# One mixer and expert layer in float32: the expert stage's weight ring re-mapped at its start, the down matrix fetched by output columns, the gate begun on quarters, the last norm taken per column block

## The chip, the cores and the metric

The kernel runs on one core of a Trainium2 chip, in one launch. The metric is the device time of that core in microseconds (us). All numbers are float32. TensorE (PE in the tables) multiplies, VectorE (DVE) and ScalarE (ACT) do the elementwise work, SyncE (SP) issues nearly all transfers.

## What is computed

One layer on 256 tokens of width 2048: a token mixer (a state-space branch and a gated delta-rule branch), a layer norm, then 32 experts of hidden width 512, of which each token takes 4, and a second layer norm.

```python
h = layer_norm(DEEPNORM_ALPHA * h + mix, ln1_g, ln1_b)
logits = h @ w_router + b_router
top_val, top_idx = lax.top_k(logits, 4); top_w = softmax(top_val)
...
gate = jnp.minimum(xb @ w_gate[e] + b_gate[e], 7.0)
up = jnp.clip(xb @ w_up[e] + b_up[e], -7.0, 7.0)
y = (gate * sigmoid(1.702 * gate) * (up + 1.0)) @ w_down[e] + b_down[e]
...
h = layer_norm(DEEPNORM_ALPHA * h + ffn, ln2_g, ln2_b)
```

The expert weights are w_gate and w_up (32 x 2048 x 512) and w_down (32 x 512 x 2048), some 403 MB, each used once.

## The kernel before

The program is written engine by engine, with semaphores between them. The mixer fills the first two thirds of the time. The change touches only the stage after it.

**The expert stage** takes the experts in 16 pairs (`PAIRS`). If no expert has more than 64 tokens (`CAP`; the flag read on every engine, `over < 1`, which holds for these inputs), each pair is done on 64 + 64 token slots, one expert in columns 0 to 63 of the array and the other in columns 64 to 127. A float32 matmul of the code is two MATMUL instructions in the trace; the counts here are of instructions. PE's order for pair i is in `sparse(i)`:

- `sgate`: two small matmuls (four instructions) lay the biases into banks 0 and 1, then `expand(0, 0, i)` multiplies by w_gate in four steps of 16 instructions (L1108);
- `sup`: `expand(1, 4, i)`, the same with w_up;
- `gather(i + 1)`: the tokens of the next pair are picked by 64 instructions (L1086) into banks 4 to 7, which ACT copies to `xg` in four quarters (`sgather`, L1454);
- `scatter(i - 1, 0, 6)`: six of the eight matmuls (two instructions each, L1165) that spread the last pair's outputs to the tokens, added to `acc` by DVE (L2050);
- `turn_hidden` (L1128), the last two scatters, `turn_weights` (L1133): transposes that ACT copies to `shT` and `pwT` (`sturn`);
- `sdown`: four steps of 16 instructions (L1142). Step k multiplies a quarter of the hidden width and adds to all four output banks, so that all banks finish in step 3; ACT then copies them to `ysb` (L1474).

In pair 0 the scatter carries b_down too (`bias_part`, L1035), and it runs in pair 1.

**The weights** come in units of 2 MB: twelve a pair (`PER_PAIR`), j = 0 to 3 of w_gate, 4 to 7 of w_up, 8 to 11 of w_down. A unit holds both experts: two rows of 2048 numbers in each of 128 partitions. Six places (`unit[0..5]`, `UNITS`) form a ring. For pair 0 there are three more, `extra`, which take j = 6, 7 and 8, so that nine units are loaded before the stage begins. From then on SP reloads in the order in which PE reads: j = 9, 10, 11 of pair 0, then all of pair 1, and so on. Unit j goes to place j % 6, and `reload_unit` waits until that place's last user was read:

```python
sp.wait_ge(unit_read[j % UNITS], 2 * i + j // UNITS - (1 if j % UNITS < 3 else 0))
```

Since SP works in order, a unit whose place isn't free holds back all later ones. PE releases a place behind the last matmul that reads it (`last.then_inc(read, 1)`).

**The end.** After the last pair's `sdown` come its eight scatters, four column blocks of token tile 0 and then four of tile 1. DVE adds each block (L2069) and takes its statistics (L2071); behind each tile `spread` makes mean, variance and reciprocal (L1866 to L1871), ACT the square root (L1402). Then DVE normalises each tile with a pass over 2048 columns (L2090) and two over 1024 (L2095), and SP stores each half (L503).

Of the kernel before, what the change touches and what calls it, by code (L numbers as in the profile page):

```python
# [12 lines left out]
ALU = mybir.AluOpType  # L13
ACT = mybir.ActivationFunctionType
# [55 lines left out]
def build(nc, x, w_in, conv_w, a_log, dt_bias, norm_w, w_dn, lam_re, lam_im, log_dt, b_re, b_im, c_re, c_im,  # L70
# [3 lines left out]
    with ExitStack() as ctx:  # L74
# [139 lines left out]
        def lnv(m, i):  # L214
            return small[:, 64 + 8 * m + i:65 + 8 * m + i]

        def top8(m, i):
            return small[:, 80 + 16 * m + 8 * i:88 + 16 * m + 8 * i]

# [55 lines left out]
        p_built, xg_done, xg_taken, y_copied, sc_done, sc_taken, sdn_done = (  # L275
            sem("p_built"), sem("xg_done"), sem("xg_taken"), sem("y_copied"), sem("sc_done"), sem("sc_taken"),
            sem("sdn_done"))
# [27 lines left out]

        def tile_rows(w):
            return w.rearrange("(k p) n -> p k n", p=P)

        block = ctx.enter_context(nc.Block())

# [2 lines left out]
        def _(sp):  # L313
# [117 lines left out]
            def load_extra(j):  # L431
                sp.dma_start(extra[j - UNITS], unit_source(j, 0)).then_inc(extra_loaded[j - UNITS], 16)
# [171 lines left out]
        def _(pe):  # L604
# [485 lines left out]
            def await_unit(j, i):  # L1090
                if isinstance(i, int) and i == 0 and UNITS <= j < UNITS + 3:
                    pe.wait_ge(extra_loaded[j - UNITS], 16)
                    return extra[j - UNITS], extra_read
                b = j % UNITS
                if isinstance(i, int) and i == 0:
                    pe.wait_ge(unit_loaded[b], 16 * (j // UNITS) + 16)
                else:
                    pe.wait_ge(unit_loaded[b], 32 * i + 16 * (j // UNITS) + (0 if b < 3 else 16))
# [26 lines left out]
            def turn_hidden(i):  # L1125
                pe.wait_ge(hb_ready, i + 1)
                for k in range(KF):
                    last = tr(ps[4][:, k * P:k * P + P], shb[:, k::KF], ident[:, :])  # L1128
                last.then_inc(htr_ready, 1)

            def turn_weights(i):
                for m in range(MT):
                    last = tr(ps[5][:, m * P:m * P + P], Pw[:, m].rearrange("p o c -> p (o c)"), ident[:, :])  # L1133
                last.then_inc(htr_ready, 1)

            def sdown(i):
                pe.wait_ge(htr_taken, 2 * i + 2)
                for k in range(KF):
                    buf, read = await_unit(8 + k, i)
                    for n in range(4):  # L1140
                        for o in range(2):
                            last = mm(ps[4 + n][CAP * o:CAP * o + CAP, :], shT[:, k, CAP * o:CAP * o + CAP],  # L1142
                                      buf[:, o, n * 512:n * 512 + 512], start=k == 0, stop=k == KF - 1)
                        if k == KF - 1 and n < 3:
                            last.then_inc(sdn_done, 1)
                    last.then_inc(read, 1)

            def scatter(i, lo, hi, more=True):
                if lo == 0:
                    pe.wait_ge(y_copied, 4 * i + 4)  # L1150
                    if more:
                        pe.wait_ge(up_taken, i + 2)
                    else:
                        pe.wait_ge(sc_taken, 8 * i)
# [15 lines left out]
            def sparse(i, first=False, more=True):  # L1170

                sgate(i)
                sup(i)
                if first:
                    turn_wt()
                if more:
                    gather(i + 1)
                if not first:
                    scatter(i - 1, 0, 6)
                pe.wait_ge(xg_taken, 4 * i + (8 if more else 4))  # L1180
                turn_hidden(i)
# [9 lines left out]
            with pe.If(over < 1):  # L1191
# [5 lines left out]
                scatter(PAIRS - 1, 0, 8, more=False)  # L1197
            with pe.If(over > 0):
                turn_tokens()
                turn_wt()  # L1200
# [11 lines left out]
        def _(act):  # L1212
# [254 lines left out]

            def sdown(i):
                for n in range(4):
                    if n < 3:  # L1470
                        act.wait_ge(sdn_done, 3 * i + n + 1)
                    else:
                        act.wait_ge(unit_read[5], 2 * i + 2)
# [20 lines left out]
            with act.If(over > 0):  # L1494
# [4 lines left out]
                    hidden(e)  # L1499
                    turn(e - 1)  # L1500
                turn(N_E - 1)
            for m in range(MT):
                root(m, MT + m)


        @block.vector
        def _(dve):
# [511 lines left out]
                    V.tensor_tensor(av, av, ps[6 + n % 2][:, :], ALU.add).then_inc(dn_taken[n % 2], 1)  # L2019

            def stake_gate(i):
                dve.wait_ge(unit_read[3], 2 * i + 1)
# [4 lines left out]
            def stake_up(i):  # L2027
                if isinstance(i, int) and i == 0:
                    dve.wait_ge(extra_read, 2)
                else:  # L2030
                    dve.wait_ge(unit_read[1], 2 * i + 1)
# [21 lines left out]
            with dve.If(over < 1):  # L2053
# [11 lines left out]
                for m in range(MT):  # L2065
                    for n in range(4):
                        av = acc[:, m, 512 * n:512 * n + 512]
                        dve.wait_ge(sc_done, 8 * (PAIRS - 1) + 4 * m + n + 1)
                        V.tensor_tensor(av, av, ps[(2, 3, 0, 1)[n]][:, :], ALU.add).then_inc(sc_taken, 1)  # L2069
                        dve.drain()  # L2070
                        V.bn_stats(stats[:, 24 * m + 6 * n:24 * m + 6 * n + 6], av)  # L2071
                    spread(m, 24 * m, 24 * m + 24)
            with dve.If(over > 0):
                add_down(-1)
                take_gate(0)
# [7 lines left out]
                for m in range(MT):  # L2083
                    for n in range(4):
                        V.bn_stats(stats[:, 24 * m + 6 * n:24 * m + 6 * n + 6], acc[:, m, 512 * n:512 * n + 512])
                    spread(m, 24 * m, 24 * m + 24)
            dve.wait_ge(ln2_loaded, 32)
            for m in range(MT):
                dve.wait_ge(root_ready, MT + m + 1)
                V.scalar_tensor_tensor(out=acc[:, m], in0=acc[:, m], scalar=lnv(m, MU), in1=ln2row[:, 0],  # L2090
                                       op0=ALU.subtract, op1=ALU.mult)
                dve.drain()
                for h in range(2):
                    half = slice(D // 2 * h, D // 2 * h + D // 2)
                    V.scalar_tensor_tensor(out=acc[:, m, half], in0=acc[:, m, half], scalar=lnv(m, RSTD),  # L2095
# [26 lines left out]
```

## Time and profile before

| | us |
|---|---|
| median of three runs | 2986.1 (2983.25 to 2987.63) |
| the profiled execution's own time | 2986.08 |
| its span in the profile | 2984.3 |
| PE busy, share of the span | 97% |
| DVE, ACT busy | 31%, 17% |
| data moved by transfers | 654.05 MB |
| expert stage, from the first expert gather to the end of the span | 1993.5 to 2984.3 |

The profile gives times from the start of the span. Busy shares are averages over stages with different limits, and matmul ends are modelled. "Idle before, releaser" names what ended an engine's idle time. The chain of waits is followed back from the last instruction to what released each step. The share of DMA is the time that packets took on the 16 transfer engines, which can come out a little over 1.

### The profile page before, as it was taken

To read this page: it belongs to the slowest core of one execution; us is meant where nothing else is said; L and a number is where in the kernel's file an instruction comes from. 1 tells how busy PE (TensorE), PEld (TensorE's weight loads), DVE (VectorE), ACT (ScalarE), POOL (GpSimd) and SP (SyncE) were. 2 spreads that over 40 slices of the span, in tenths; PEclk is the share of its full clock that TensorE was granted. 3 is DMA by queue.
4 is the path that set the end of the run, shared out by engine and by line. 5 is a ranking of instruction groups with operands and counts; after the bars stand their busy time and mean duration, and the time that the engine had idled before them with its cause. 6 is when DMAs were issued, how large, how long until landed. Compare 5 with 4: busy or idle time off the path is not lost.

```text
span 2984.3 us, 47457 instructions
## 1 busy us (share of the span) xinstructions
PE 2900.1 (97%) x19639; PEld 2086.5 (70%) x19639; DVE 912.0 (31%) x2066; ACT 517.6 (17%) x809; POOL 100.5 (3%) x179
## 2 busy tenths in 40 slices
PE   8999999999999999999999999999999999999996
PEld 7888788888888888888888888873444444444442
DVE  1433424424334307777730000130121112111214
ACT  2221222222212132111010000121111111112110
POOL 2010011000100000000000000000000000000000
PEclk9999999999999999999999999999999999999998
DMA  6243342332434524244347665258899999999996
GB/s 195 81 131 99 98 125 91 101 123 80 138 94 113 154 95 136 92 127 128 122 145 218 197 194 171 112 204 361 362 422 422 422 422 422 422 422 422 422 422 261
DMA packets 325775, 654.05 MB, mean 219 GB/s; under 512 B 45232, under 2 KB 274736, under 8 KB 275440
## 3 DMA queue, kind: packets, MB, share of 16 engines
q1 hardware_dynamic: 325616, 651.61, 59.4%
q8 instruction: 139, 2.28, 0.3%
q14 instruction: 20, 0.16, 0.0%
HBM read 649.49 MB, written 2.10 MB: 218 GB/s over the span
## 4 chain that ended last, share of the span: by engine, by line
PE 58%; issue 16%; DVE 12%; DMA 6%; DVEq 2%; ACT 1%; POOLq 1%; POOL 1%; SPq 1%; ACTq 0%
PE bank L938 11%; PE bank L632 10%; PE bank L1108 9%; PE bank L1142 7%; DMA arena<-in_w_up_dram 6%; DVE arena L1759 4%; PE bank L1086 4%; PE bank L972 4%; PE bank L1165 4%; DVE arena L1761 3%; DVE arena L1763 3%; PE bank L706 1%; PE bank L724 1%; PE bank L717 1%; PE bank L1119 1%
## 5 line engine op out<-in xcount | busy, mean ns | idle before, releaser
L632 PE MATMUL bank<-arena 128*128 128x256 f32 x4096 | 934.0, 383 | 0.0
L632 PEld LDWEIGHTS bank<-arena 128*128 128x128 f32 x4096 | 765.3, 190 | 112.6 <-issue 8.0
L1108 PE MATMUL bank<-arena 128*64 128x512 f32 x2048 | 447.0, 595 | 6.2 <-DMA arena<-in_w_up_dram 6.2
L1108 PEld LDWEIGHTS bank<-arena 128*64 128x64 f32 x2048 | 145.1, 137 | 306.1 <-issue 290.1
L938 PE MATMUL bank<-arena 128*128 128x256 f32 x1536 | 331.8, 379 | 0.0
L938 PEld LDWEIGHTS bank<-arena 128*128 128x128 f32 x1536 | 291.8, 190 | 39.9 <-issue 0.3
L1142 PE MATMUL bank<-arena 128*64 128x512 f32 x1024 | 223.3, 594 | 7.7 <-ACT masks L1466 7.7
L877 PE MATMUL bank<-arena 128*128 128x256 f32 x1024 | 223.5, 380 | 0.0
L877 PEld LDWEIGHTS bank<-arena 128*128 128x128 f32 x1024 | 194.0, 190 | 27.3 <-issue 1.0
L1142 PEld LDWEIGHTS bank<-arena 128*64 128x64 f32 x1024 | 72.1, 137 | 148.5 <-issue 137.0
L2023 DVE TENSOR_SCALAR arena<-bank 128x512 f32<-128x512 f32 x16 | 11.1, 692 | 473.7 <-PE bank L1108 473.7
L1454 ACT ACTIVATE arena<-bank,small 128x128 f32<-128x128 f32 x256 | 96.2, 456 | 224.5 <-PE bank L1086 224.5
L1759 DVE TENSOR_TENSOR arena<-arena 128x256 f32<-128x256 f32 x256 | 124.2, 485 | 32.5 <-issue 15.5
L1086 PEld LDWEIGHTS bank<-arena 128*128 128x128 f32 x1024 | 116.9, 194 | 12.1 <-issue 11.4
L1086 PE MATMUL bank<-arena 128*128 128x128 f32 x1024 | 119.8, 278 | 0.7 <-ACTq L1410 0.7
L1165 PE MATMUL bank<-arena,masks 128*128 128x512 f32 x256 | 117.0, 596 | 2.5 <-DVEq L2037 1.8
L2050 DVE TENSOR_TENSOR arena<-arena,bank 128x512 f32<-128x512 f32 x120 | 82.4, 688 | 105.2 <-PE bank L1165 105.0
L972 PE MATMUL bank<-arena 128*128 128x256 f32 x512 | 114.0, 381 | 0.0
L1551 DVE TENSOR_SCALAR arena<-bank,cw 128x256 f32<-128x256 f32 x64 | 28.0, 480 | 256.5 <-PE bank L632 255.8
L972 PEld LDWEIGHTS bank<-arena 128*128 128x128 f32 x512 | 96.2, 190 | 12.5
L1761 DVE TENSOR_TENSOR arena<-arena 128x128 f32 x256 | 82.8, 323 | 43.5 <-issue 43.5
L1557 DVE SCALAR_TENSOR_TENSOR arena<-bank,cw,arena 128x255 f32<-128x255 f32 (+2 forms) x192 | 83.7, 477 | 16.5 <-issue 16.4
(307 smaller groups left out, 2001.4 us busy)
## 6 DMA issues: line engine op xcount, KB each, us to landing
arena<-in_w_in_dram SPq DMA_DIRECT2D x72, 2048.0 KB, 8.7
arena<-in_w_up_dram SPq DMA_DIRECT2D x64, 2048.0 KB, 15.9
arena<-in_w_gate_dram SPq DMA_DIRECT2D x64, 2048.0 KB, 13.4
arena<-in_w_down_dram SPq DMA_DIRECT2D x64, 2048.0 KB, 20.6
arena<-in_w_dn_out_dram SPq DMA_DIRECT2D x16, 2048.0 KB, 8.5
arena<-in_w_glu_b_dram SPq DMA_DIRECT2D x8, 2048.0 KB, 8.2
arena<-in_w_glu_a_dram SPq DMA_DIRECT2D x8, 2048.0 KB, 8.3
arena<-in_w_mix_out_dram SPq DMA_DIRECT2D x8, 2048.0 KB, 13.7
```

The lines of the kernel that those rows point to most:

```text
L632: last = mm(ps[bank][:, ct * T:ct * T + T], ring[:, buf, k, ct * P:ct * P + P], rhs[:, k, :], start=k == 0, stop=k == KD - 1)
L877: last = mm(ps[bank][:, ct * T:ct * T + T], ring[:, n % 2, k, ct * P:ct * P + P], oT[:, half * KD + k, :], start=half == 0 and ct == 0 and ...
L938: last = mm(ps[3 - 3 * odd + b][:, ct * T:ct * T + T], ring[:, buf, k, ct * P:ct * P + P], rhs[:, k, :], start=k == 0, stop=k == KD - 1)
L972: last = mm(ps[bank][:, 0:SC], mg[:, k, m * P:m * P + P], mixw[r][:, k, :], start=k == 0, stop=k == KD - 1)
L1086: last = mm(ps[4 + b][:, k * P:k * P + P], h1[:, m, 4 * b + k], Psel[:, m].rearrange("p o c -> p (o c)"), start=m == 0, stop=m == MT - 1)
L1108: last = mm(ps[bank][CAP * o:CAP * o + CAP, :], xg[:, 4 * q + k, CAP * o:CAP * o + CAP], w[:, o, k], start=False, stop=q == 3 and k == 3, ...
L1142: last = mm(ps[4 + n][CAP * o:CAP * o + CAP, :], shT[:, k, CAP * o:CAP * o + CAP], buf[:, o, n * 512:n * 512 + 512], start=k == 0, stop=k ...
L1165: last = mm(ps[bank][:, :], pwT[:, (n // 4) * P:(n // 4) * P + P], ysb[:, (n % 4) * 512:(n % 4) * 512 + 512], start=not biased, stop=True, ...
L1454: last = A(xg[:, k, :], ps[4 + b][:, P * j:P * j + P], ACT.Identity, scale=gqk[:, k:k + 1], bias=bqk[:, k:k + 1])
L1759: V.tensor_tensor(prod, prev.unsqueeze(2).to_broadcast([P, 2, 2, NJ]), rot, ALU.mult)
L1761: V.tensor_tensor(cur, cur, prod[:, 0], ALU.add)
L1763: V.tensor_tensor(cur, cur, prod[:, 1], ALU.add)
```

## The change

Four edits, all in the expert stage and its end.

1. **Places.** `place_of(j, i)` and `earlier_uses(j, i)` take the place of `j % UNITS` and of the two counts, on SP, PE, DVE and ACT. Units 9, 10, 11 of pair 0 go to places 0, 1, 2 (before 3, 4, 5), and unit j of every later pair to (j + 3) % 6.
2. **The down matrix.** Unit 8 + n of w_down holds 512 output columns, n * 512 and on, of all 512 hidden rows, where it held a quarter of the hidden rows with all 2048 columns. `sdown` is `down_columns(i, n)` for n = 0 to 3: 16 instructions into bank 4 + n alone. ACT's copy of a bank waits for that unit's release (`sdn_done` is gone). The first step waits for `shT` alone, the others for `pwT` too. The hidden transposes read contiguous columns (`shb[:, k * P:...]`).
3. **The gate** waits for the quarters of `xg` one by one, and the bias matmuls before it for none.
4. **The end.** In the last pair `scatter_columns(i, n)` stands behind `down_columns(i, n + 1)`: the two token tiles of one column block. DVE takes the blocks in that order, then makes the statistics of both tiles in one go (`ln_pair`), and the first normalising pass starts before the square root is there.

```diff
+        def place_of(j, i):
+            if isinstance(i, int) and i == 0:
+                return j if j < UNITS else j - UNITS - 3
+            return (j + 3) % UNITS
+
+        def earlier_uses(j, i):
+            if isinstance(i, int) and i == 0:
+                return 0 if j < UNITS else 1
+            return 2 * i + j // UNITS - (0 if place_of(j, i) < 3 else 1)
...
                 if kind == 2:
-                    return w_down[ds(2 * i, 2)].rearrange("o (p k) n -> p o k n", k=KF)[:, :, quarter, :]
+                    return (w_down[ds(2 * i, 2)].rearrange("o (k p) n -> p (o k) n", p=P)
+                            [:, :, F_E * quarter:F_E * quarter + F_E])
...
             def load_unit(j, i):
-                sp.dma_start(unit[j % UNITS], unit_source(j, i)).then_inc(unit_loaded[j % UNITS], 16)
+                b = place_of(j, i)
+                to = unit[b] if j < 8 else unit[b].rearrange("p o (k n) -> p (o k) n", k=KF)
+                sp.dma_start(to, unit_source(j, i)).then_inc(unit_loaded[b], 16)
...
-                sp.wait_ge(unit_read[j % UNITS], 2 * i + j // UNITS - (1 if j % UNITS < 3 else 0))
+                sp.wait_ge(unit_read[place_of(j, i)], earlier_uses(j, i))
...
             def expand(bank, first, i):
                 for q in range(4):
                     j = first + q
+                    if bank == 0:
+                        pe.wait_ge(xg_taken, 4 * i + q + 1)
...
             def sgate(i):
-                pe.wait_ge(xg_taken, 4 * i + 4)
...
-                    last = tr(ps[4][:, k * P:k * P + P], shb[:, k::KF], ident[:, :])
+                    last = tr(ps[4][:, k * P:k * P + P], shb[:, k * P:k * P + P], ident[:, :])
...
+            def down_columns(i, n):
+                pe.wait_ge(htr_taken, 2 * i + 1 + (n > 0))
+                buf, read = await_unit(8 + n, i)
+                w = buf.rearrange("p o (k n) -> p o k n", k=KF)
+                for k in range(KF):
+                    for o in range(2):
+                        last = mm(ps[4 + n][CAP * o:CAP * o + CAP, :], shT[:, k, CAP * o:CAP * o + CAP], w[:, o, k],
+                                  start=k == 0, stop=k == KF - 1)
+                last.then_inc(read, 1)
+
             def sdown(i):
-                pe.wait_ge(htr_taken, 2 * i + 2)
...
+            def scatter_columns(i, n):
+
+                pe.wait_ge(y_copied, 4 * i + n + 1)
+                for m in range(MT):
+                    j = 2 * n + m
+                    pe.wait_ge(sc_taken, 8 * i + max(j - 3, 0))
+                    mm(ps[(2, 3, 0, 1)[j % 4]][:, :], pwT[:, m * P:m * P + P], ysb[:, n * 512:n * 512 + 512],
+                       start=True, stop=True).then_inc(sc_done, 1)
...
                 turn_weights(i)
-                sdown(i)
+                if more:
+                    sdown(i)
+                else:
+                    down_columns(i, 0)
+                    for n in range(1, 4):
+                        down_columns(i, n)
+                        scatter_columns(i, n - 1)
+                    scatter_columns(i, 3)
...
+            dve.drain()
+            for m in range(MT):
+                V.bn_aggr(small[:, 64 + 8 * m + MU:64 + 8 * m + MU + 2], stats[:, 24 * m:24 * m + 24])
+            dve.drain()
+            V.tensor_scalar(ln_pair(RINV), ln_pair(VAR), LN_EPS, None, ALU.add)
+            dve.drain()
+            V.reciprocal(ln_pair(RINV), ln_pair(RINV))
```

On SP the first reloads of the stage stood like this before (L432 is unit 8 of pair 0, L429 the reloads of units 9, 10, 11 of pair 0; `unit3_free` and its like are the counts of reads of a place; the last figures are partitions x pieces x numbers in a piece):

```order
L432 DMA arena<-in_w_down_dram 128x2x2048 [waits resid_done]
L469 TENSOR_LOAD flag [waits flag_ready]
L469 ISA x2
L470 COMPARE_AND_BRANCH
L429 DMA arena<-in_w_down_dram 128x2x2048 [waits unit3_free]
L429 DMA arena<-in_w_down_dram 128x2x2048 [waits unit4_free]
L429 DMA arena<-in_w_down_dram 128x2x2048 [waits unit5_free]
```

and now:

```order
L448 DMA arena<-in_w_down_dram 128x8x512 [waits resid_done]
L485 TENSOR_LOAD flag [waits flag_ready]
L485 ISA x2
L486 COMPARE_AND_BRANCH
L444 DMA arena<-in_w_down_dram 128x8x512 [waits unit0_free]
L444 DMA arena<-in_w_down_dram 128x8x512 [waits unit1_free]
L444 DMA arena<-in_w_down_dram 128x8x512 [waits unit2_free]
```

The three reloads wait for places that are read three units sooner, and each piece in memory is 512 numbers (2 KB) instead of 2048 (8 KB), eight in a partition instead of two.

On PE the last pair ended like this before (L1133 is `turn_weights`, L1142 `sdown`, L1165 the scatter):

```order
L1133 MATMUL bank<-ident,arena 128x128 x2
L1142 MATMUL bank<-arena 64x512 [waits unit2_loaded,htr_taken]
L1142 MATMUL bank<-arena 64x512 x7
L1142 MATMUL bank<-arena 64x512 [waits unit3_loaded]
L1142 MATMUL bank<-arena 64x512 x7
L1142 MATMUL bank<-arena 64x512 [waits unit4_loaded]
L1142 MATMUL bank<-arena 64x512 x7
L1142 MATMUL bank<-arena 64x512 [waits unit5_loaded]
L1142 MATMUL bank<-arena 64x512 x7
L1165 MATMUL bank<-arena,masks 128x512 [waits sc_taken,y_copied]
L1165 MATMUL bank<-arena,masks 128x512 x3
L1165 MATMUL bank<-arena,masks 128x512 [waits sc_taken] x4
```

and now, from its second column block on (L1156 is `down_columns`, L1170 `scatter_columns`):

```order
L1156 MATMUL bank<-arena 64x512 [waits unit0_loaded,htr_taken]
L1156 MATMUL bank<-arena 64x512 x7
L1170 MATMUL bank<-arena,masks 128x512 [waits sc_taken,y_copied]
L1170 MATMUL bank<-arena,masks 128x512 [waits sc_taken]
L1156 MATMUL bank<-arena 64x512 [waits unit1_loaded,htr_taken]
L1156 MATMUL bank<-arena 64x512 x7
L1170 MATMUL bank<-arena,masks 128x512 [waits sc_taken,y_copied]
L1170 MATMUL bank<-arena,masks 128x512 [waits sc_taken]
```

Six of the eight scatters have moved ahead of the end: two stand behind the second, the third and the last down step each, and two more at the very end.

## Rows read from the trace of the kernel before

**Rows 1.** The page, part 2: the span in 40 slices of 74.6 us.

```profile
PE   8999999999999999999999999999999999999996
PEclk9999999999999999999999999999999999999998
DMA  6243342332434524244347665258899999999996
GB/s 195 81 131 99 98 125 91 101 123 80 138 94 113 154 95 136 92 127 128 122 145 218 197 194 171 112 204 361 362 422 422 422 422 422 422 422 422 422 422 261
```

**Rows 2.** The chain of waits, 2360 to 2460: start us, us, what.

```profile
2366.13 7.04 PE bank L1108 x32
...
2373.31 17.56 DMA arena<-in_w_up_dram
...
2390.92 3.65 PE bank L1108 x16
...
2432.98 17.59 DMA arena<-in_w_up_dram
```

**Rows 3.** Stretches: from:to, length, busy times, granted clock, DMA share, GB/s.

```profile
1622.00:1630.00 8.00, 8.00 (x39) 7.04 (x38) 0.00 (x0) 0.00 (x0) 0.00 (x0) 1.00 1.09 351
...
2056.00:2108.00 52.00, 52.00 (x238) 21.29 (x234) 7.89 (x18) 8.98 (x21) 0.00 (x0) 1.00 1.01 422
2108.00:2118.00 10.00, 9.54 (x33) 3.58 (x34) 2.13 (x4) 0.96 (x2) 0.00 (x0) 1.00 0.18 75
2120.00:2900.00 780.00, 768.70 (x3704) 328.49 (x3702) 130.31 (x273) 130.39 (x301) 0.00 (x0) 1.00 1.01 422
```

**Rows 4.** SP's instructions in order of time: start us, us, line, what.

```profile
2021.89 6.89 SPq L429 DMA_DIRECT2D arena<-in_w_down_dram  x3
2029.21 24.48 SPq L429 DMA_DIRECT2D arena<-in_w_gate_dram  x4
```

**Rows 5.** PE in order of time, pairs 0 to 3.

```profile
1993.54 8.75 PE L1086 MATMUL bank<-arena 128*128 128x128 f32 x64 [0.67 <-ACTq L1410]
2003.88 1.98 PE L1119 MATMUL bank<-arena,masks 32*128 32x512 f32 x4 [1.59 <-ACT arena L1454]
...
2045.99 13.96 PE L1142 MATMUL bank<-arena 128*64 128x512 f32 x64 [0.73 <-ACT masks L1466]
...
2114.82 13.95 PE L1142 MATMUL bank<-arena 128*64 128x512 f32 x64 [0.46 <-ACT masks L1466]
...
2187.54 1.98 PE L1119 MATMUL bank<-arena,masks 32*128 32x512 f32 x4
...
2246.39 1.98 PE L1119 MATMUL bank<-arena,masks 32*128 32x512 f32 x4
```

**Rows 6.** Issue to landing, least/median/most: L432 at 2001.7 (8 KB pieces).

```profile
DMA to landing us min/median/max: 7.5/7.5/7.5
```

**Rows 7.** The same for L366, 1087 to 1500 (24 transfers, 1 KB pieces).

```profile
DMA to landing us min/median/max: 8.1/8.6/9.7
```

**Rows 8.** PE in order of time, the end.

```profile
2928.06 3.65 PE L1108 MATMUL bank<-arena 128*64 128x512 f32 x16 [0.87 <-DMA arena<-in_w_up_dram]
...
2941.78 13.95 PE L1142 MATMUL bank<-arena 128*64 128x512 f32 x64 [0.46 <-ACT masks L1466]
2956.42 7.16 PE L1165 MATMUL bank<-arena,masks 128*128 128x512 f32 x16 [0.69 <-ACT arena L1474]
```

**Rows 9.** DVE in order of time, the end.

```profile
2957.58 0.69 DVE L2069 TENSOR_TENSOR arena<-arena,bank 128x512 f32<-128x512 f32 x1 [15.76 <-PE bank L1165]
...
2958.97 0.67 DVE L2069 TENSOR_TENSOR arena<-arena,bank 128x512 f32<-128x512 f32 x1
...
2969.83 0.26 DVE L1866 BATCH_NORM_AGGREGATE small<-small 128x2 f32<-128x24 f32 x1
...
2971.40 2.35 DVE L2090 SCALAR_TENSOR_TENSOR arena<-arena,small 128x2048 f32<-128x2048 f32 x1 [0.78 <-ACTq L1402]
```

More of the change, by code:

```diff
@@ L215, in lnv, with ln_pair @@
             return small[:, 64 + 8 * m + i:65 + 8 * m + i]
+        def ln_pair(i):
+            return small[:, 64:80].rearrange("p (m i) -> p m i", i=8)[:, :, i]
         def top8(m, i):
@@ L274, in build @@
         sel_ready, pos_ready, flag_ready = sem("sel_ready"), sem("pos_ready"), sem("flag_ready")
-        p_built, xg_done, xg_taken, y_copied, sc_done, sc_taken, sdn_done = (
-            sem("p_built"), sem("xg_done"), sem("xg_taken"), sem("y_copied"), sem("sc_done"), sem("sc_taken"),
-            sem("sdn_done"))
+        p_built, xg_done, xg_taken, y_copied, sc_done, sc_taken = (
+            sem("p_built"), sem("xg_done"), sem("xg_taken"), sem("y_copied"), sem("sc_done"), sem("sc_taken"))
         x_loaded = [sem(f"x_tile{m}_loaded") for m in range(MT)]
@@ L428, in load_unit @@
             def load_unit(j, i):
-                sp.dma_start(unit[j % UNITS], unit_source(j, i)).then_inc(unit_loaded[j % UNITS], 16)
+                b = place_of(j, i)
+                to = unit[b] if j < 8 else unit[b].rearrange("p o (k n) -> p (o k) n", k=KF)
+                sp.dma_start(to, unit_source(j, i)).then_inc(unit_loaded[b], 16)
             def load_extra(j):
-                sp.dma_start(extra[j - UNITS], unit_source(j, 0)).then_inc(extra_loaded[j - UNITS], 16)
+                to = extra[j - UNITS] if j < 8 else extra[j - UNITS].rearrange("p o (k n) -> p (o k) n", k=KF)
+                sp.dma_start(to, unit_source(j, 0)).then_inc(extra_loaded[j - UNITS], 16)
             def reload_unit(j, i):
-                sp.wait_ge(unit_read[j % UNITS], 2 * i + j // UNITS - (1 if j % UNITS < 3 else 0))
+                sp.wait_ge(unit_read[place_of(j, i)], earlier_uses(j, i))
                 sp.sem_inc(load_free, 1)
@@ L1093, in await_unit @@
                     return extra[j - UNITS], extra_read
[L1094 to L1098, printed above, removed]
+                b = place_of(j, i)
+                pe.wait_ge(unit_loaded[b], 16 * earlier_uses(j, i) + 16)
                 return unit[b], unit_read[b]
@@ L1134, in turn_weights, with scatter @@
                 last.then_inc(htr_ready, 1)
-            def sdown(i):
-                pe.wait_ge(htr_taken, 2 * i + 2)
[L1138 to L1148, printed above, removed]
+            def down_columns(i, n):
[7 more added lines that the diff above has]
+                last.then_inc(read, 1)
+            def sdown(i):
+                for n in range(4):
+                    down_columns(i, n)
[6 more added lines that the diff above has]
+                       start=True, stop=True).then_inc(sc_done, 1)
+            def scatter(i, lo, hi):
                 if lo == 0:
                     pe.wait_ge(y_copied, 4 * i + 4)
[L1151 to L1154, printed above, removed]
+                    pe.wait_ge(up_taken, i + 2)
                 biased = isinstance(i, int) and i == 0
@@ L1184, in sparse @@
                 turn_weights(i)
-                sdown(i)
+                if more:
[3 more added lines that the diff above has]
+                    for n in range(1, 4):
+                        down_columns(i, n)
+                        scatter_columns(i, n - 1)
+                    scatter_columns(i, 3)
             pe.wait_ge(xhat_done, MT)
@@ L1196, in _ @@
                 sparse(PAIRS - 1, more=False)
-                scatter(PAIRS - 1, 0, 8, more=False)
             with pe.If(over > 0):
@@ L1469, in sdown @@
                 for n in range(4):
-                    if n < 3:
-                        act.wait_ge(sdn_done, 3 * i + n + 1)
+                    if isinstance(i, int) and i == 0 and n == 0:
+                        act.wait_ge(extra_read, 3)
                     else:
-                        act.wait_ge(unit_read[5], 2 * i + 2)
+                        act.wait_ge(unit_read[place_of(8 + n, i)], earlier_uses(8 + n, i) + 1)
                     nc.scalar.copy(ysb[:, n * 512:n * 512 + 512], ps[4 + n][:, :]).then_inc(y_copied, 1)
@@ L1501, in _ @@
                 turn(N_E - 1)
-            for m in range(MT):
-                root(m, MT + m)
+            act.wait_ge(rv_ready, MT + 1)
+            A(ln_pair(RSTD), ln_pair(RINV), ACT.Sqrt)
+            act.drain()
+            act.sem_inc(root_ready, 1)
         @block.vector
@@ L2021, in stake_gate @@
             def stake_gate(i):
-                dve.wait_ge(unit_read[3], 2 * i + 1)
+                dve.wait_ge(unit_read[place_of(3, i)], earlier_uses(3, i) + 1)
                 V.tensor_scalar(sgb, ps[0][:, :], LIMIT, None, ALU.min)
@@ L2030, in stake_up @@
                 else:
-                    dve.wait_ge(unit_read[1], 2 * i + 1)
+                    dve.wait_ge(unit_read[place_of(7, i)], earlier_uses(7, i) + 1)
                 V.tensor_scalar(shb, ps[1][:, :], LIMIT, -LIMIT, ALU.min, ALU.max)
@@ L2064, in _ @@
                 add_scatter(PAIRS - 2)
-                for m in range(MT):
-                    for n in range(4):
+                for n in range(4):
+                    for m in range(MT):
+                        j = 2 * n + m
                         av = acc[:, m, 512 * n:512 * n + 512]
-                        dve.wait_ge(sc_done, 8 * (PAIRS - 1) + 4 * m + n + 1)
-                        V.tensor_tensor(av, av, ps[(2, 3, 0, 1)[n]][:, :], ALU.add).then_inc(sc_taken, 1)
+                        dve.wait_ge(sc_done, 8 * (PAIRS - 1) + j + 1)
+                        V.tensor_tensor(av, av, ps[(2, 3, 0, 1)[j % 4]][:, :], ALU.add).then_inc(sc_taken, 1)
                         dve.drain()
                         V.bn_stats(stats[:, 24 * m + 6 * n:24 * m + 6 * n + 6], av)
-                    spread(m, 24 * m, 24 * m + 24)
             with dve.If(over > 0):
@@ L2085, in _ @@
                         V.bn_stats(stats[:, 24 * m + 6 * n:24 * m + 6 * n + 6], acc[:, m, 512 * n:512 * n + 512])
-                    spread(m, 24 * m, 24 * m + 24)
+            dve.drain()
+            for m in range(MT):
+                V.bn_aggr(small[:, 64 + 8 * m + MU:64 + 8 * m + MU + 2], stats[:, 24 * m:24 * m + 24])
[3 more added lines that the diff above has]
+            V.reciprocal(ln_pair(RINV), ln_pair(RINV))
+            dve.drain()
+            dve.sem_inc(rv_ready, 1)
             dve.wait_ge(ln2_loaded, 32)
             for m in range(MT):
-                dve.wait_ge(root_ready, MT + m + 1)
                 V.scalar_tensor_tensor(out=acc[:, m], in0=acc[:, m], scalar=lnv(m, MU), in1=ln2row[:, 0],
@@ L2092, in _ @@
                 dve.drain()
+                if m == 0:
+                    dve.wait_ge(root_ready, MT + 1)
                 for h in range(2):
```

## The prediction

> **What bounds the kernel now.** I read the page's slices first. In the last third, from the 29th slice on, the transfers run at 422 GB/s in every full slice, while PE is also busy nine tenths [rows 1]: two resources are near their limit, and the page can't say which sets the pace. The chain of waits can. Once in each pair it leaves PE for some 17.6 us and goes over a transfer of w_up: 2373.31, then 2432.98, so once in 59.67 us [rows 2]. Twelve units at 422 GB/s are 12 x 2.097 MB / 422 = 59.63 us: the pair lasts as long as its weights take to arrive. PE alone needs less. In an early pair, in which it waits for no transfer, it goes from one bias step to the next in 2246.39 - 2187.54 = 58.85 us [rows 5]. So the stage is bound by the transfers, and PE has 0.8 us of slack in a pair. Whatever makes the stream of weights longer is paid in full; whatever makes PE shorter is lost, but at the two ends.
>
> Where does the stream begin to bind? The stretches show it full from 2056 to 2108, nearly idle from 2108 to 2118 (share 0.18), and then full at 422 GB/s to 2900 [rows 3]. The hole is there because PE is late: pair 1 has the scatter with b_down, its down step begins only at 2114.82 [rows 5], and unit 2 of pair 2 needs the place that the first down unit of pair 1 gives back some 3.5 us later. From this point 162 units (10 of pair 2, 12 in each of pairs 3 to 14, 8 of pair 15) flow without a hole to PE's last wait for a transfer, at 2928.06 [rows 8]. Behind it comes the tail, which is PE and DVE alone: last down step, scatters, statistics, norm.
>
> So the time is the restart of the stream, plus 162 units, plus the tail. Each edit is put to these three terms. The sum is made against the profiled execution, 2986.08 us (span 2984.3); the median of the runs is 2986.1, so the difference carries over unchanged.
>
> **Places: 0.** Units 9 to 11 of pair 0 were issued at 2021.89, when unit 3 had been read [rows 4]. They now wait for unit 0, three steps earlier: the 16 instructions of a step take 3.5 us (13.96 / 4) [rows 5], so 10.5 us sooner. But units 0, 1, 2 of pair 1 come next [rows 4], and behind them unit 3, which needs unit 9's place, before and after alike, and that is read only in pair 0's down step. The stream, sooner or later, stands at this point. Nothing in pair 0 or 1 waited for a transfer (the idle before its steps is for ACT [rows 5]), so the earlier arrival has no taker. What covers it is the hole of 2108 to 2118, about 8 us of idle transfers; were it gone, up to 10.5 us would count, a rival below.
>
> **Gate on quarters, first down step without pwT: -2.4 us on the restart.** PE stood 1.59 us before the first bias matmul at 2003.88, for ACT's last quarter [rows 5]; the bias no longer waits and takes 1.9 us, in which that quarter is copied: -1.6. The down step waited 0.73 us in pair 0 and 0.46 in pair 1 for the copy to `pwT` [rows 5]. In pair 0 the copy to `shT` stands just ahead of it and still has to be awaited, so I take -0.3; in pair 1 -0.5. PE reaches pair 1's down step 2.4 us sooner and the stream restarts 2.4 us sooner. In pairs 2 to 14 the same 0.5 us is hidden by the transfers, as is a gate wait that had long been met.
>
> **Down units of 2 KB pieces: +22.4 us on the stream.** A unit was 256 pieces of 8 KB, 16 for each of 16 engines; now it is 1024 pieces of 2 KB, 64 for each. No large transfer in this trace has 2 KB pieces, so I bound it from both sides of the size. With 8 KB the stream holds 422 GB/s: a piece costs 16 x 8192 / 422 = 310.6 ns. With 1 KB (w_glu and w_mix, queued behind each other) it holds 351 GB/s [rows 3]: 16 x 1024 / 351 = 46.7 ns. The line through both is 9.0 ns a piece plus 0.0368 ns a byte; 2 KB then cost 84.4 ns, a unit 64 x 84.4 = 5.40 us against 16 x 310.6 = 4.97, so +0.43 us. Transfers that run alone are the further bound: 7.5 us with 8 KB [rows 6], 8.1 to 9.7 (most often 8.6) with 1 KB [rows 7], for 112 pieces more per engine. The 48 more of a 2 KB unit would be 48/112 of 0.6 to 2.2 us, 0.26 to 0.94 us. A gain is not excluded by a row, but both sizes put the larger piece ahead; the bound below is 0. I take 0.43, from full-rate rows like those of this stage. Of the 162 units 4 in each of pairs 2 to 14 are down units: 52 x 0.43 = +22.4. Those of pairs 0 and 1 (8 x 0.43 = 3.4 us) fall into the hole, those of pair 15 lie behind the last wait, where PE reaches each some 4 us after it has landed. The Trainium skill says otherwise: DMA: Bandwidth & Descriptors, Specifications, puts full rate at transfers of 512 B and more, by which 2 KB pieces would be free.
>
> SP's issues stay as many, and the 16 instructions of a step keep their shape: 0. With 61.4 us a pair PE's slack grows to some 3 us, so ACT's copies, now spread over the down steps, wait for nobody.
>
> **The tail: -4.9 us.** Before, from the down step at 2941.78 [rows 8] to the first normalising pass at 2971.40 [rows 9]. Now: down starts 0.5 us sooner, 2941.3. Four steps are 13.9 us; two pairs of scatters stand among them, and the eight scatters took 7.16 us, 0.86 each without the last one's drain [rows 8], so 4 x 0.86 = 3.4; the last step ends at 2958.6. The scatters of block 2 follow at once, while ACT copies block 3. DVE took its first block 1.16 us behind the first scatter (2957.58 against 2956.42), and a block, add and statistics, takes 1.39 us (2958.97 - 2957.58), longer than a scatter [rows 8, 9]. DVE has four blocks left where it had eight: 2958.6 + 1.2 + 5.6 = 2965.4. From aggregation to reciprocal it is for one tile 2971.40 - 2969.83 less 0.78 for the root, 0.8 [rows 9], plus 0.3 for the second tile: the first pass starts at 2966.5. The root is made under that pass of 2.35 us [rows 9]. 2966.5 - 2971.4 = -4.9; the passes and stores behind it are the same.
>
> **Sum.** -2.4 + 22.4 - 4.9 = +15.1 us: 2986.1 + 15.1 = **3001.2 us**.
>
> **The rivals.**
> - *Pieces of 2 KB are free.* Each engine would have enough in its queue to hide what a piece costs beyond its bytes. Then -2.4 - 4.9 = -7.3: 2978.8 us, faster. It decides below 7.3 / 52 = 0.14 us a unit, 79.9 ns a piece. This is what the page's 512 B would give. Against it: full queues of 1 KB pieces, half that size, hold 351 GB/s and not 422 [rows 3]. For it: none of the rows is of 2 KB. Chance 0.17.
> - *Most of it hidden, not all*: 0.14 to 0.26 us a unit, between that point and the lower bound of the lone transfers, +0 to +6.2: 2986 to 2992. Chance 0.08.
> - *The early reloads carry through*: the hole closes, since the stream has more of a lead than I read from the ring, and the 10.5 us of the first reloads count at the end. +15.1 - 10.5 = +4.6: 2990.7. Against it is the wait for unit 9's place, in both orders. Chance 0.06.
> - *Rows 8 KB apart cost memory time too.* A piece is now one quarter of a matrix row, and a unit touches 1024 rows. With the most that lone 1 KB transfers took, 0.94 us, 52 x 0.94 - 7.3 = +41.6: 3027.7 us. Beyond 0.65 us (3012.6) I call it this case. Against it: the 351 GB/s are of matrices whose rows are 8 KB apart as well. Chance 0.10. The Trainium skill, DMA: Bandwidth & Descriptors, Latency and other measured facts, reports such losses for row pitches from 2 MiB up; no row here shows one.
> - *The edit is not what it says*: the order of SP shows 128x8x512, so the transfers are cut as the diff has it; only a joining of pieces in hardware could undo this, which is the first rival.
>
> **How the numbers follow.** The forecast, 0.26 to 0.65 us a unit (+6.2 to +26.5, 2992 to 3013), has 0.59. The range reaches down into the free case and a little into the dear one, and leaves out some 0.1 of the former and 0.07 of the latter: 2979 to 3015. A measurement of this kernel can tell about 0.2%, 6 us. Faster by more than that needs less than 0.03 us a unit: 0.13 of the first rival's 0.17. Within it: the rest, 0.04, the half-hidden case 0.08 and the early reloads 0.06, together 0.18. Slower: 0.59 + 0.10 = 0.69.
>
> **What would show it.** Right: full stretches of the stage near 410 GB/s (12 units in 61.35 us), a period of some 61.4 us between the w_up waits in the chain, PE's wait per pair grown from under 1 to some 3 us; the hole before pair 1's down step still there; PE's last wait at about 2928 + 20 = 2948; the first normalising pass 4.4 us nearer to the last down step. Wrong: 422 GB/s and 59.7 us a pair (pieces are free), no hole near 2110 (the early reloads count), or under 400 GB/s (rows cost).

## The result and the profile after

Five runs of the changed kernel have a median of 3000.87 us (2999.21 to 3001.55); the kernel before, five runs, 2983.25 us (2981.47 to 2987.63). The ratio is 1.0056, 95% interval 1.0041 to 1.0071: slower, by 17.6 us of the medians. The forecast was 3001.2 us and slower, +15.1.

The page of the kernel after, its first line and its slices of 75 us, answers to [rows 1]:

```profile
span 2999.1 us, 47575 instructions
...
PE   8999999999999999999999999999999999999997
...
DMA  7233242242334534334347665268999999999997
GB/s 206 85 114 113 86 141 85 86 141 85 113 113 100 154 100 129 111 113 141 113 141 225 199 209 178 101 245 346 365 411 412 408 405 412 412 411 405 408 412 285
```

Where 422 GB/s stood in every full slice there are now 405 to 412. The busy share of the transfer engines is as high as before: they work as much and bring less.

The chain of waits of the kernel after, 2360 to 2460 (start us, us, what), against [rows 2]:

```profile
2373.97 19.91 DMA arena<-in_w_up_dram
...
2393.93 3.65 PE bank L1123 x16
...
2435.42 19.89 DMA arena<-in_w_up_dram
...
2455.36 3.65 PE bank L1123 x16
```

The wait for w_up ends at 2393.93 and again at 2455.36: a pair is 61.43 us, where it was 59.67.

The stretches of the kernel after (columns as in [rows 3]):

```profile
2108.00:2118.00 10.00, 10.00 (x43) 3.38 (x44) 1.38 (x2) 1.19 (x3) 0.00 (x0) 1.00 0.26 83
2120.00:2900.00 780.00, 750.22 (x3611) 317.40 (x3608) 126.91 (x269) 127.11 (x295) 0.00 (x0) 1.00 1.03 409
```

The hole before pair 1's down step is still there, and behind it 409 GB/s take the place of 422. PE's busy time in the same 780 us fell from 768.70 to 750.22 us: it waits. In the kernel before, 5.3 us of PE's waits in this stretch ended with a transfer of w_up and 6.0 with ACT's copy to `pwT`; now it is 29.8 us, all for w_up.

PE in order of time, kernel after, first pairs, against [rows 5], and the end, against [rows 8]:

```profile
1990.99 9.86 PE L1102 MATMUL bank<-arena 128*128 128x128 f32 x64 [0.47 <-DVEq L1989]
2000.79 1.98 PE L1133 MATMUL bank<-arena,masks 32*128 32x512 f32 x4
...
2040.82 15.50 PE L1156 MATMUL bank<-arena 128*64 128x512 f32 x64 [0.46 <-ACT arena L1492]
...
2110.63 13.95 PE L1156 MATMUL bank<-arena 128*64 128x512 f32 x64
...
2942.30 3.65 PE L1123 MATMUL bank<-arena 128*64 128x512 f32 x16 [1.31 <-DMA arena<-in_w_up_dram]
2947.28 3.65 PE L1123 MATMUL bank<-arena 128*64 128x512 f32 x16 [1.32 <-DMA arena<-in_w_up_dram]
...
2960.43 7.09 PE L1156 MATMUL bank<-arena 128*64 128x512 f32 x32
...
2978.44 3.70 PE L1170 MATMUL bank<-arena,masks 128*128 128x512 f32 x8
```

Four of these starts cut the stage into the three terms of the forecast. *Start* is from the first gather to pair 1's down step, where the stream of weights restarts. *Stream* is from there to PE's last wait for a transfer. *Tail* is from there to the end of the span.

| us | before | after | difference | forecast |
|---|---|---|---|---|
| start | 2114.82 - 1993.54 = 121.28 | 2110.63 - 1990.99 = 119.64 | -1.6 | -2.4 |
| stream | 2928.06 - 2114.82 = 813.24 | 2947.28 - 2110.63 = 836.65 | +23.4 | +22.4 |
| tail | 2984.3 - 2928.06 = 56.24 | 2999.1 - 2947.28 = 51.82 | -4.4 | -4.9 |
| sum | 990.76 | 1008.11 | +17.35 | +15.1 |

What lies ahead of the first gather is the same code in both and differed by 2.6 us between these two executions; over all runs shown below the first gather began between 1987.8 and 1996.2. A difference of single executions carries that scatter, which is why the terms are read inside the stage.

DVE in order of time, kernel after, against [rows 9]:

```profile
2979.61 0.69 DVE L2100 TENSOR_TENSOR arena<-arena,bank 128x512 f32<-128x512 f32 x1 [2.65 <-PE bank L1170]
...
2985.27 0.39 DVE L2118 BATCH_NORM_AGGREGATE small<-small 128x2 f32<-128x24 f32 x2
...
2986.27 2.35 DVE L2127 SCALAR_TENSOR_TENSOR arena<-arena,small 128x2048 f32<-128x2048 f32 x1
```

Four blocks of 1.4 us are left when the last two scatter pairs arrive, and the first normalising pass follows the aggregation at once: no idle time for the root stands before it, as it did in [rows 9].

### The profile page after: what moved, and what is told of

It reads as the page before. It is cut to its first block, busy times and chain, and to the rows that moved or that the text cites. A ratio compares the mean times of both kernels' runs of the same rounds, so it can differ in the third digit from the quotient of the medians.

```text
span 2999.1 us, 47575 instructions
## 1 busy us (share of the span) xinstructions
PE 2902.9 (97%) x19639; PEld 2083.3 (69%) x19639; DVE 912.3 (30%) x2062; ACT 517.3 (17%) x808; POOL 100.5 (3%) x179
## 4 chain that ended last, share of the span: by engine, by line
PE 56%; issue 16%; DVE 12%; DMA 9%; DVEq 2%; POOLq 1%; POOL 1%; ACT 1%; SPq 1%; ACTq 0%
PE bank L954 11%; PE bank L648 10%; DMA arena<-in_w_up_dram 9%; PE bank L1156 7%; PE bank L1123 7%; DVE arena L1789 4%; PE bank L1102 4%; PE bank L988 4%; PE bank L1187 3%; DVE arena L1791 3%; DVE arena L1793 3%; PE bank L722 1%; PE bank L740 1%; PE bank L733 1%; PE bank L1133 1%
## 5 line engine op out<-in xcount | busy, mean ns | idle before, releaser
L1156 PE MATMUL bank<-arena 128*64 128x512 f32 x1024 | 225.2, 597 | 0.5 <-ACT arena L1492 0.5
L1156 PEld LDWEIGHTS bank<-arena 128*64 128x64 f32 x1024 | 72.1, 138 | 142.0 <-issue 141.3
L1102 PEld LDWEIGHTS bank<-arena 128*128 128x128 f32 x1024 | 118.0, 195 | 11.9 <-issue 11.4
L1187 PE MATMUL bank<-arena,masks 128*128 128x512 f32 x240 | 109.8, 596 | 1.8 <-DVEq L2067 1.8
```

The costliest lines, as they stand in the source:

```text
L1102: last = mm(ps[4 + b][:, k * P:k * P + P], h1[:, m, 4 * b + k], Psel[:, m].rearrange("p o c -> p (o c)"), start=m == 0, stop=m == MT - 1)
L1187: last = mm(ps[bank][:, :], pwT[:, (n // 4) * P:(n // 4) * P + P], ysb[:, (n % 4) * 512:(n % 4) * 512 + 512], start=not biased, stop=True, ...
```

## The experiments

The theory: the loss is a fixed time for each piece of a down unit, paid in 52 units; start and tail keep small gains. Its rivals: PE's new order or new waits; rows far apart; a threshold in the piece size; early reloads that hid part of the loss. Each run is told by its ratio to the kernel before on the same chip. The stream term of each is read from its own trace, as in the table above.

**e1: the change with whole rows.**

```diff
                 if kind == 2:
-                    return (w_down[ds(2 * i, 2)].rearrange("o (k p) n -> p (o k) n", p=P)
-                            [:, :, F_E * quarter:F_E * quarter + F_E])
+                    return w_down[ds(2 * i, 2)].rearrange("o (p k) n -> p o k n", k=KF)[:, :, quarter, :]
...
-                to = unit[b] if j < 8 else unit[b].rearrange("p o (k n) -> p (o k) n", k=KF)
+                to = unit[b]
...
```

> The changed kernel, but each down unit is fetched in whole rows of 8 KB again (the transfers of the kernel before), while PE, ACT and DVE do what the change has them do. The weights so multiplied are not the reference's. Theory (the piece size costs 0.43 us a down unit, 52 of them on the path): 22 us less than the changed kernel, ratio to before about 0.9976 (some 2976 to 2979 us where before is 2983), 422 GB/s and 59.7 us a pair. Rival (the time comes from PE's new order, its new waits or the new places): stays near 3001 us.

Measured: 2976.52 us, ratio 0.9969 (0.9957 to 0.9981). PE, stretch and end of this run:

```profile
2120.00:2900.00 780.00, 768.15 (x3705) 327.17 (x3702) 130.31 (x273) 130.78 (x302) 0.00 (x0) 1.00 1.01 422
```

```profile
2114.01 11.38 PE L1155 MATMUL bank<-arena 128*64 128x512 f32 x52
...
2927.36 3.65 PE L1122 MATMUL bank<-arena 128*64 128x512 f32 x16 [1.31 <-DMA arena<-in_w_up_dram]
```

The stream is 2927.36 - 2114.01 = 813.35 us, as before the change (813.24). Every instruction of PE, ACT and DVE is the change's; the source and destination patterns of the down units' transfers are not. So the whole loss is in how the down units are fetched, and the rest of the change is faster than the kernel before.

**e3: the columns alone, on the kernel before.** `unit_source`, the two destinations, the transposes, `sdown` and ACT's waits for it are as in the change; places, gate and end are the old ones, and the down step still waits for both copies.

```diff
             def sdown(i):
                 pe.wait_ge(htr_taken, 2 * i + 2)
-                for k in range(KF):
-                    buf, read = await_unit(8 + k, i)
...
+                for n in range(4):
+                    buf, read = await_unit(8 + n, i)
+                    w = buf.rearrange("p o (k n) -> p o k n", k=KF)
```

> The kernel before with the down matrix by output columns and nothing else of the change: old places, gate behind all four quarters, both copies awaited before the down step, old end. Theory: 52 x 0.43 = 22.4 us more than before, some 3005 to 3007 us, ratio 1.0075. The tail and the start give nothing. Rival (part of the loss comes from the other edits): less than 17 us more.

Measured: 3007.76 us, ratio 1.0075 (1.0061 to 1.0088), which is 22.6 us over the 2985.2 of the kernel before measured beside it. Its stream is 2953.50 - 2117.09 = 836.41 us, within 0.3 us of the change's 836.65. From both sides then: with whole rows the change gains, and the columns alone lose all and more.

**e2: pieces of 2 KB, but near each other.** The eight pieces of a partition are every second 2 KB of 32 KB of one expert's matrix, instead of eight rows 1 MB apart.

```diff
...
+                    return (w_down[ds(2 * i + quarter // 2, 1)].rearrange("o (p k) n -> p (o k n)", k=KF)
+                            .rearrange("p (c t n) -> p c t n", t=2, n=512)[:, :, quarter % 2, :])
...
```

> The changed kernel with down units of 2 KB pieces that lie 4 KB apart, all of a partition's eight pieces within 32 KB of memory, instead of in eight rows 1 MB apart. The data is each weight once, in another order, so the product is not the reference's. Theory (a fixed time for each piece, wherever it lies): the same as the changed kernel, near 3001 us, 410 GB/s, 61.4 us a pair. Rival (rows far apart cost time in memory): down to some 2979 us, or in between as far as it holds.

Measured: 2998.89 us, ratio 1.0046 (1.0033 to 1.0059), an interval that overlaps with that of the change.

```profile
2120.00:2900.00 780.00, 750.18 (x3617) 317.08 (x3614) 124.84 (x265) 127.28 (x295) 0.00 (x0) 1.00 1.03 410
```

```profile
2113.27 12.24 PE L1156 MATMUL bank<-arena 128*64 128x512 f32 x56
...
2949.58 3.65 PE L1123 MATMUL bank<-arena 128*64 128x512 f32 x16 [1.33 <-DMA arena<-in_w_up_dram]
```

The stream is 836.31 us against 836.65. Where the rows lie costs nothing here; that they are short costs all. The Trainium skill, DMA: Bandwidth & Descriptors, Latency and other measured facts, tells of losses in copies between HBM tensors whose partitions lie 2 MiB and more apart. This case doesn't test that: its neighbouring partitions lie 8 KB apart, and the 1 MB is between the pieces of one partition.

**e5 and e6: pieces of 1 KB and of 4 KB**, the same edit with n=256 and n=1024.

> The changed kernel with down units of 1 KB pieces, 2 KB apart (other weights than the reference's, each once). Theory (9 ns a piece plus its bytes): a down unit is 128 x 46.7 = 5.98 us, 1.0 us more than whole rows; 52 of them: 52.5 us over the whole-row version of the change (2976.5), so about 3029 us, ratio to before 1.0147, down stretches at 351 GB/s. Rival (2 KB lies below a threshold, above and below it the rate is level): near the changed kernel, 3001.

Measured: 3031.32 us, ratio 1.0169 (1.0153 to 1.0184).

```profile
2120.00:2900.00 780.00, 729.62 (x3476) 303.04 (x3472) 121.80 (x258) 120.51 (x278) 0.00 (x0) 1.00 1.05 395
```

```profile
2107.47 13.95 PE L1156 MATMUL bank<-arena 128*64 128x512 f32 x64
...
2975.13 3.65 PE L1123 MATMUL bank<-arena 128*64 128x512 f32 x16 [1.36 <-DMA arena<-in_w_up_dram]
```

> The changed kernel with down units of 4 KB pieces, 8 KB apart (other weights than the reference's, each once). Theory: 32 x (9.0 + 150.8) = 5.11 us a unit, 0.14 more than whole rows, 52 x 0.14 = 7.5 us over the whole-row version (2976.5): about 2984 us, ratio 0.9994. Rival (threshold between 2 and 8 KB): either 2977 or 3001.

Measured: 2983.72 us, ratio 1.0002 (0.9993 to 1.0011).

```profile
2120.00:2900.00 780.00, 763.45 (x3674) 324.02 (x3672) 130.25 (x273) 129.25 (x299) 0.00 (x0) 1.00 1.02 418
```

```profile
2107.91 13.95 PE L1156 MATMUL bank<-arena 128*64 128x512 f32 x64
...
2928.72 3.65 PE L1123 MATMUL bank<-arena 128*64 128x512 f32 x16 [1.31 <-DMA arena<-in_w_up_dram]
```

With these the price has four points. The last column is the third over the second, for each of the 16 engines:

| piece | more pieces per engine and unit than whole rows | stream us over 813.35, by 52 units | ns for each more piece |
|---|---|---|---|
| 4 KB | 16 | (820.81 - 813.35) / 52 = 0.143 | 9.0 |
| 2 KB | 48 | (836.31 - 813.35) / 52 = 0.442 | 9.2 |
| 1 KB | 112 | (867.66 - 813.35) / 52 = 1.044 | 9.3 |

It is one straight line: 9 ns a piece. There is no threshold between 1 and 8 KB. The four traces with whole rows up to the last pair (before, e1, e4, e8) have streams of 813.07 to 813.35 us, so the scatter of a stream moves the 9.0 of the first line by some 0.3 ns and the others by less.

The traces show the price where it is paid, too. A stretch in which the down units arrive, in the kernel before, the kernel after and e5 (8, 2 and 1 KB), and, in the last line, one of the kernel after in which gate and up units do:

```profile
2394.00:2408.00 14.00, 14.00 (x86) 10.39 (x83) 7.09 (x13) 6.44 (x17) 0.00 (x0) 1.00 1.01 422
```

```profile
2396.00:2410.00 14.00, 14.00 (x85) 9.86 (x82) 6.40 (x12) 6.01 (x16) 0.00 (x0) 1.00 1.05 387
```

```profile
2402.00:2418.00 16.00, 16.00 (x93) 10.93 (x90) 7.14 (x14) 6.60 (x17) 0.00 (x0) 1.00 1.10 348
```

```profile
2416.00:2432.00 16.00, 16.00 (x72) 5.18 (x70) 0.00 (x0) 2.34 (x4) 0.00 (x0) 1.00 1.01 421
```

A unit of 2.097 MB at 387 GB/s is 5.42 us and at 348 it is 6.03: 0.45 and 1.06 us over the 4.97 at 422. The 409 GB/s of the long stretch are an average of 387 in the down units and some 422 in the others.

**e7: the change with the old places.**

```diff
-            if isinstance(i, int) and i == 0:
-                return j if j < UNITS else j - UNITS - 3
-            return (j + 3) % UNITS
+            return j % UNITS
```

(`earlier_uses` takes the old counts.)

> The changed kernel with the old places (j % 6 and the old counts), all else as in the change. Theory: the first reloads are issued 10.5 us later and nobody waits for it, since the stream stands before pair 0's down step and before pair 1's either way: the same as the changed kernel within 2 us, 3001. Rival (the early reloads carry through and hid part of the loss): up to 10.5 us slower, 3011.

Measured: 2996.29 us (2995.93 to 3001.19), ratio 1.0053 (1.0039 to 1.0067), against 1.0056 for the change. SP in this run:

```profile
2018.71 6.89 SPq L442 DMA_DIRECT2D arena<-in_w_down_dram  x3
```

and in the kernel after:

```profile
2006.80 6.89 SPq L444 DMA_DIRECT2D arena<-in_w_down_dram  x3
2016.90 33.17 SPq L444 DMA_DIRECT2D arena<-in_w_gate_dram  x4
```

The first reloads do come 10 us sooner in the change, counted from each run's first gather (2018.71 - 1992.80 = 25.9 us against 2006.80 - 1990.99 = 15.8). But the four gate units behind them then take 33 us to issue (24 in [rows 4]), since the fourth waits for pair 0's down step. PE's rows of e7:

```profile
2110.69 13.95 PE L1154 MATMUL bank<-arena 128*64 128x512 f32 x64
...
2947.34 3.65 PE L1121 MATMUL bank<-arena 128*64 128x512 f32 x16 [1.32 <-DMA arena<-in_w_up_dram]
```

A stream of 836.65 us, that of the change to the hundredth. The interval, 11.6 to 20.0 us over the kernel before, excludes the rival's 3011. The places are worth nothing.

**e8: the gate on quarters alone, on the kernel before** (the waits of `expand` and `sgate`, as in the change's diff).

> The kernel before with the gate begun on quarters and nothing else. Theory: 1.6 us sooner at the restart of the stream, so 1.6 us less than before at most, within what the measurement can tell; and a stretch of 3.4 us at half clock in the first pairs, which costs 1.7 us, can take it back. The version with columns in the last pair alone (2975.2) should then be some 5 us below this one: that is the tail. Rival (the quarters bring most of that version's gain): 2978 or less.

Measured: 2980.98 us, ratio 0.9994 (0.9984 to 1.0004): no difference that can be told from nothing. A gain of 1 to 2 us is neither shown nor excluded by the times. The lower end of the interval is 2978.6 us, so the rival, 2978 or less, is just outside it. In its trace the idle 1.59 us before the first bias matmul of [rows 5] is gone, but pair 0's down step takes 15.30 us where the kernel before has 13.96: TensorE's clock, told in the last section.

**e4: whole rows in pairs 0 to 14, columns in the last pair.** `sdown` is the old one but in the last pair, and SP's loop ends one pair sooner, so that the last pair's units can be fetched in another way.

```diff
+        def by_columns(i):
+            return isinstance(i, int) and i == PAIRS - 1
...
-                if kind == 2:
+                if kind == 2 and by_columns(i):
                     return (w_down[ds(2 * i, 2)].rearrange("o (k p) n -> p (o k) n", p=P)
                             [:, :, F_E * quarter:F_E * quarter + F_E])
+                if kind == 2:
+                    return w_down[ds(2 * i, 2)].rearrange("o (p k) n -> p o k n", k=KF)[:, :, quarter, :]
```

> The changed kernel with whole rows of 8 KB in pairs 0 to 14 and columns of 2 KB pieces in the last pair alone, where the end needs them and where the transfers bind no more. Computes the reference. Theory: the start and the tail keep their gain, the stream loses nothing: 2983 - 7 = 2976 us, ratio 0.9976, faster than both kernels. Rival (the tail's gain was not there or is eaten by the last pair's four dearer units): no faster than before.

Measured: 2975.16 us, ratio 0.9969 (0.9958 to 0.998): faster than both kernels, and 10 us below the median of the one before measured beside it.

```profile
2108.22 13.95 PE L1175 MATMUL bank<-arena 128*64 128x512 f32 x64 [0.46 <-ACT masks L1511]
...
2921.39 3.65 PE L1131 MATMUL bank<-arena 128*64 128x512 f32 x16 [0.58 <-DMA arena<-in_w_up_dram]
...
2934.54 7.09 PE L1165 MATMUL bank<-arena 128*64 128x512 f32 x32
```

Its stream is 2921.39 - 2108.22 = 813.17 us, and from there to the end of its span (2973.2) are 51.8 us, the tail of the change: a shorter start (118.9 us) and the new tail without the loss between them. Since `sdown` waits for both copies in pairs 0 to 14, its start has the gate on quarters alone. The last pair's four dearer units cost nothing, as PE reaches them late.

## Why the prediction was right

**The bound.** It rested on the transfers' pace of a pair, 59.63 us by their rate, against 58.85 us of PE alone. e1 shows it: the pattern of the transfers moves the stream by 23.3 us (836.65 against 813.35) with PE's work unchanged, while the 0.46 us that PE saves in each pair shows nowhere in the stream (e1 has that saving and 813.35 us, the kernel before 813.24). The saving turns into waiting: from 2120 to 2900 PE waits 11.9 us for w_up in e1, where the kernel before waits 5.3 for w_up and 6.0 for ACT.

**The price of a piece**, the term that decided. No row had 2 KB pieces in number, and the value was a straight line between full queues of 1 KB and 8 KB: 0.43 us a unit. Measured are 23.4 / 52 = 0.45. The lower bound of nothing, and with it the rival that short pieces are free, has fallen, by e5, e2 and e6 at three sizes. The Trainium skill, DMA: Bandwidth & Descriptors, Specifications, gives 512 B as the least size for full rate. The runs don't agree: at 1 KB, twice that, a unit takes 1.04 us more than its 4.97. The Trainium skill, DMA: Bandwidth & Descriptors, Why small descriptors are slow, has a fixed overhead of some 3 cycles a packet. At the 850 MHz that the page gives for the fabric this is, as an estimate, 3.5 ns; the runs have 9. What makes up the 9 ns no run here shows.

**The count of 52.** It came from the order of the ring: from the restart in pair 1 to the last wait in pair 15. The chain gives the price of a unit in another way, from the pairs in the middle: (61.43 - 59.67) / 4 = 0.44 us, and 23.4 / 0.44 is 53. In the chains of e6 and e5 the pairs are 60.24 and 63.86 us, so 0.14 and 1.05 us a unit: the prices of the table, without the 52 in them. That the last pair's four cost nothing is shown by e4. That those of pairs 0 and 1 fall into the hole was not tried by itself; the hole in the trace of after (share 0.26 from 2108 to 2118) says so.

**The places at nothing**: right, shown by e7.

**The start**: -2.4 forecast, -1.6 in the traces. The waits went as said: 1.59 us gone before the bias matmuls, 0.73 us down to 0.46 before pair 0's down step, 0.46 down to nothing before pair 1's, and 0.2 us more around the short transposes, together -2.5. TensorE's clock, told below, took 0.9 of it back. Before and after:

```profile
2005.79 29.38 PE L1108 MATMUL bank<-arena 128*64 128x512 f32 x128
```

```profile
2002.70 27.69 PE L1123 MATMUL bank<-arena 128*64 128x512 f32 x128
```

The same gate and up steps are 1.7 us shorter after the change, while its first gather is 1.1 us longer (9.86 against 8.75) and pair 0's down step 1.5 (15.50 against 13.96). In the variants of the change without a slow stretch behind the gather (e1, e6, e7) the term is 117.7 to 117.9 us, with one it is 119.6 to 120.2 (after, e2, e5). So the size of this term is known to some 2 us and no better.

**The tail**: -4.9 forecast, -4.4 measured. The down step began 0.6 us sooner (13.15 us behind the last wait against 13.72), and the half microsecond was lost between down steps and scatters: from the first down step to the last scatters it is 2978.44 - 2960.43 = 18.0 us, for which the forecast had 17.3. (Of the eight scatters four, not six, stand ahead of the last down step's end; the other four follow it, the x8 row of 3.70 us. The forecast's sum had that right.)

**The half-hidden case and the dear case** had prices of 0.14 to 0.26 and over 0.65 us a unit; 0.45 excludes both.

**The signs** came out as listed or nearly so: 409 GB/s for 410, 61.43 us for 61.4, the hole still there, PE's last wait at 2947.28 for 2948, and waits of 1.32 and 1.33 us for w_up in a pair, 2.65 for "some 3". The first normalising pass is 3.8 us nearer to the last down step (25.84 us against 29.62), where 4.4 were forecast: the half microsecond above.

**How close it was.** The mechanism and the sizes held, and the three terms missed by 0.8, 1.0 and 0.5 us, all to the same side. That 3001.2 meets the measured 3000.87 within 0.3 us is luck: the forecast started from 2986.1, and the five runs of the kernel before have 2983.25. The loss is 17.6 us, 2.5 more than forecast.

## What to carry to other kernels

Where a stage is bound by its weights, look at the length of the contiguous run before anything else: with PE waiting, a layout of the work that cuts a transfer's rows into four is paid for in every unit, however well it serves the engines. The price can be read beforehand from two sizes at full rate in the same trace. And a layout that only the end of the kernel needs should be used only at the end, where the transfers are ahead.

## What the runs showed of the hardware

TensorE's granted clock falls to its lower level, 1.2 of 2.4 GHz, for some microseconds near the start of the stage, and where it falls differs from run to run. All ten traces have one in the first gather, behind a wait of 2.6 us for DVE; the gather takes 8.75 us (before) to 10.27 us (e2), where the gather of the next pair takes 7.31. Six have a second one behind it. The stretch 2040 to 2045 of the kernel after and 2006 to 2011 of the kernel before, each with a mean granted clock of 0.66 (2042 to 2044 and 2008 to 2010, inside them, read 0.50):

```profile
2040.00:2045.00 5.00, 4.54 (x16) 1.41 (x16) 0.00 (x0) 0.86 (x2) 0.00 (x0) 0.66 0.02 8
```

```profile
2006.00:2011.00 5.00, 5.00 (x18) 1.43 (x16) 0.00 (x0) 0.00 (x0) 0.00 (x0) 0.66 0.47 198
```

Ahead of the first, PE had waited 1.59 us and 0.46 us for ACT around short transposes; ahead of the second 1.59 us. The down step that it meets takes 15.50 us, where the next takes 13.95: 1.55 us, as much as the gate on quarters was to give. e1, e6 and e7, with the same waits, had no such stretch there, and neither had the kernel before, with 1.60 and 0.73 us ahead of the same step. So the fall can't be forecast from the waits alone, and a gain of 1 or 2 us at such a place is within what it gives or takes.
